# A weight tile rounded before the tanh in the feed-forward's first steps, the key norm's parts ahead of the query's, and in the attention an eviction moved up and a weight split moved behind the loop

## The reference

```python
for l in range(DEPTH):                       # two layers
    h = rmsnorm(x, g_mix[l])
    ...
    if l == 1:
        hk = rmsnorm(x, g_kv)                # the same x under a second gain
        kvf = hk @ w_kvf                     # keys, values, forget logits
        p = h @ w_in_b[0]                    # queries, and the memory's queries
        mix = forgetting_attention(q, k_sh, v_sh, cum_logf)   # 12 heads
    mem_o = memory_attention(q_mem, mem_k, mem_v)             # 4 heads
    x = x + jnp.concatenate([mix, mem_o], axis=-1) @ w_out[l]
    x = x + conv_ffn(rmsnorm(x, g_ffn[l]), w_up[l], w_dw_f[l], b_dw_f[l], w_down[l])

def conv_ffn(h, w_up, w_dw, b_dw, w_down):
    u = causal_dwconv(h @ w_up, w_dw, b_dw)  # three taps over time
    gate, val = jnp.split(u, 2, axis=-1)
    return (jax.nn.silu(gate) * val) @ w_down
```

## Time and profile before

| what | value |
|---|---|
| median of 3 runs | 1224.46 us (1223.63 to 1225.26) |
| the profiled execution's own time | 1224.42 us |
| its span, first to last instruction | 1222.6 us |
| PE busy | 1176.3 us, 96% of the span |
| DVE busy | 854.8 us, 70% |
| ACT busy | 599.6 us, 49% |
| transfers | mean 166 GB/s, the 16 DMA engines 45% busy with the stream |
| mean granted TensorE clock | 0.99 of full |

### The profile page before, as it was taken

The page is one execution under the profiler, slowest core; times in us unless marked ns, Lnnn a source line. Parts: engine busy times, 40 slices in busy tenths (PEclk is TensorE's granted clock), DMA queues, the critical chain, the costliest instruction groups (busy, mean ns, idle before and its releaser), DMA issues.

```text
span 1222.6 us, 19215 instructions
## 1 busy us (share of the span) xinstructions
PE 1176.3 (96%) x7966; PEld 1054.6 (86%) x7966; DVE 854.8 (70%) x1310; ACT 599.6 (49%) x933; POOL 24.6 (2%) x40
## 2 busy tenths in 40 slices
PE   6989998999999999899999999999999999999997
PEld 6958898999899779899999978878799789999885
DVE  5995678787767657887778856665676257777664
ACT  6525545545554435455545334444553245565552
POOL 3000000000000000000000000000000000000000
PEclk9999999999999999999999999999999999999998
DMA  9634444555443314455544544544575522322351
GB/s 378 209 108 158 173 173 174 199 179 179 183 173 118 125 69 173 140 205 177 198 176 152 208 158 149 203 156 155 206 276 207 211 99 99 106 103 104 136 192 50
DMA packets 31398, 202.81 MB, mean 166 GB/s; under 512 B 4048, under 2 KB 4176, under 8 KB 8784
## 3 DMA queue, kind: packets, MB, share of 16 engines
q1 hardware_dynamic: 31312, 201.58, 45.3%
HBM read 198.18 MB, written 1.05 MB: 163 GB/s over the span
## 4 chain that ended last, share of the span: by engine, by line
PE 82%; DVE 9%; ACT 4%; issue 2%; DMA 1%; DVEq 0%; ACTq 0%; POOLq 0%; SPq 0%; POOL 0%
PE bank L792 24%; PE bank L793 23%; PE bank L794 23%; DVE WL L1687 3%; ACT WH L1318 2%; DVE work L1882 2%; PE bank L1292 1%; PE bank L1275 1%; PE bank L1218 1%; PE bank L1182 1%; PE bank L926 1%; PE bank L1006 1%; DMA xn<-cmpw 1%; PE bank L1266 1%; DVE work L1834 1%
## 5 line engine op out<-in xcount | busy, mean ns | idle before, releaser
L1687 DVE TENSOR_TENSOR WL<-RAW,WH 128x2048 fp32r<-128x2048 f32 x172 | 394.8, 2298 | 154.4 <-ACT WH L1318 153.2
L1318 ACT ACTIVATE WH<-RAW 128x2048 fp32r<-128x2048 f32 x172 | 328.5, 1912 | 215.5 <-PE bank L794 207.6
L792 PE MATMUL bank<-XH,WH 128*128 128x256 f32 x1264 | 363.1, 287 | 19.5 <-DVE WL L1903 11.9
L793 PE MATMUL bank<-XL,WH 128*128 128x256 f32 x1264 | 359.5, 284 | 0.0
L794 PE MATMUL bank<-XH,WL 128*128 128x256 f32 x1264 | 359.4, 284 | 0.0
L792 PEld LDWEIGHTS bank<-XH,WH 128*128 128x128 f32 x1264 | 244.4, 193 | 23.6 <-DVE XL L1896 11.8
L793 PEld LDWEIGHTS bank<-XL,WH 128*128 128x128 f32 x1264 | 244.5, 193 | 0.6
L794 PEld LDWEIGHTS bank<-XH,WL 128*128 128x128 f32 x1264 | 244.3, 193 | 0.0
L792 PE MATMUL bank<-WH,MH 128*128 128x512 f32 (+1 forms) x480 | 182.3, 380 | 3.7 <-DVE work L1758 2.7
L793 PE MATMUL bank<-WL,MH 128*128 128x512 f32 (+1 forms) x480 | 179.9, 375 | 0.0
L794 PE MATMUL bank<-WH,ML 128*128 128x512 f32 (+1 forms) x480 | 179.5, 374 | 0.0
(11 more groups left out here) (294 smaller groups left out, 1471.3 us busy)
## 6 DMA issues: line engine op xcount, KB each, us to landing
RAW<-wstream SPq DMA_DIRECT2D x173, 1024.0 KB, 4.8
con<-cmpw SPq DMA_DIRECT2D x6, 512.0 KB, 5.7
xn<-cmpw SPq DMA_DIRECT2D x4, 512.0 KB, 7.6
con<-consts SPq DMA_DIRECT2D x1, 1617.0 KB, 6.7
work<-xT_in SPq DMA_DIRECT2D x1, 1024.0 KB, 4.9
x<-x_in SPq DMA_DIRECT2D x1, 1024.0 KB, 10.8
work<-mem_in SPq DMA_DIRECT2D x1, 1024.0 KB, 15.8
xn<-memT_in SPq DMA_DIRECT2D x1, 1024.0 KB, 13.2
```

What stands on the lines that cost most here:

```text
L792: mm(o, ah, bh, start=start, stop=False)
L793: mm(o, ah, bl, start=False, stop=False)
L1318: act_fn(WH[:, t % RING, :], RAW[:, t % RING, :], ACT.Copy).then_inc(w_rounded, 1)
L1687: tt(WL[:, t % RING, :], RAW[:, t % RING, :], WH[:, t % RING, :].bitcast(F32), ALU.subtract).then_inc(w_split, 1)
```

## The change

Four places are edited; every operation stays, and PE's and SP's lists are the same as before.

1. In `ffn`, ACT and DVE no longer take the extra tile in steps 0 and 1 (the term `0 < 2 * s + q < 2 * LAG` goes). In steps 0, 1 and 2 (s <= LAG) ACT rounds one more tile before it waits for DVE's gate taps and does the tanh; DVE's split of it stands behind the eviction of the value product.
2. In `high` and `low`, with two gains, all four blocks of the half go under the first gain and then all four under the second; ACT waits before each pair of the second for DVE's pair of the first (part_done).
3. In the attention's slot 11, DVE's eviction of qm,1 stands ahead of the maxima and the copy instead of behind them.
4. In slot 16 DVE doesn't split a weight tile any more. The split comes in the call of `enter` that follows the loop.

```diff
             def high(n, h, gains=(0,)):
-                for j in (2 * h, 2 * h + 1):
-                    ready(act, ("tr", n, j))
-                    for dst, _, name in [norms[n][g] for g in gains]:
+                for at, (dst, _, name) in enumerate([norms[n][g] for g in gains]):
+                    for j in (2 * h, 2 * h + 1):
+                        ready(act, ("tr", n, j))
+                        if at:
+                            act.wait_ge(part_done, j + 1)
                         for kk in range(2):
...
                     for q, name in enumerate(("fg", "fv")):
-                        upto_n(at + 1 + q + (0 < 2 * s + q < 2 * LAG))
+                        upto_n(at + 1 + q)
                         is_free(act, (name, l, s))
...
                         if q == 0:
+                            if s <= LAG:
+                                upto_n(at + 2)
                             act.wait_ge(*dve_a.next())
...
             def low(n, h, gains=(0,)):
-                for j in (2 * h, 2 * h + 1):
-                    dve.wait_ge(*hi_a.next(2 * len(gains)))
-                    for g in gains:
-                        hi, dst, name = norms[n][g]
+                for g in gains:
+                    hi, dst, name = norms[n][g]
+                    for j in (2 * h, 2 * h + 1):
+                        dve.wait_ge(*hi_a.next(2))
                         for kk in range(2):
...
-                    if s in pieces:
+                    if s in pieces and s < n:
                         upto(pieces[s][0])
+                    if s in pieces and pieces[s] == (("qm", 1), 1):
+                        by_head(("qm", 1), q_mem)
...
-                        elif name == "qm":
-                            by_head((name, j), q_mem)
...
                         scaled((name, l, s), u[:, 2 * q:2 * q + 2, :])
-                        upto_n(at + 1 + q + (0 < 2 * s + q < 2 * LAG))
+                        upto_n(at + 1 + q)
```

## The result

The changed kernel takes 1207.14 us (median of four executions, 1207.06 to 1208.61) against 1224.86 us before (1223.63 to 1225.33). The ratio is 0.986, with a 95% interval of 0.9843 to 0.9877: 17.7 us less. The profiled execution took 1207.18 us, 17.24 less than the profiled one before (1224.42), its span is 1205.4, and the mean granted clock rose from 0.990 to 0.996.

A forecast was written before the change was run, and what follows sets the result against it. PE, busy 96% of the span, was taken as the bound, each long wait paid twice, as idle time and slow clock. Terms 10.0 + 0.5 + 3.6 + 3.2 = 17.3 us off 1224.4 gave 1207.1, range 1204.8 to 1213.

The forecast's parts named there:

- The feed-forward: Both passes at fv3: the wait for its split (3.42 us) and the slow clock behind it (1.58) go, 10.0 us.
- The norm: Layer 1's norm: keys' parts ready 1.4 us earlier, but q1,0's split limits PE's start; 0.5 us gained.
- Slot 11: Attention, o1,0: earlier eviction of qm,1 starts PE 2.0 us sooner and saves 1.55 of slow clock; 3.6 us together.
- Slot 16: Attention's end: without the split ahead of the copies PE's outputs start 1.5 us earlier, plus 1.7 for the clock; 3.2 us.
- rival D: An early gain, above all the attention's 6.8 us, is used up by a later wait; 1213.9 us, chance 0.04.
- Rival B: A remaining wait of 1.1 us, at the attention's end or q1,0, still lowers the clock; 1208.7 us, chance 0.20.
- C: The feed-forward's split is late still, at worst with about no gain there; 1209 to 1217.1 us, chance 0.12.
- E: Feed-forward steps 0 to 2, both passes: the rounding ahead holds up the tanh; slower, up to 1227.9 us, chance 0.02.
- that rule: Attention's end: transposes don't count as busy, so the clock falls once more; gain 15.6 us instead of 17.3.

The follow-up runs named there:

- no_ffn: Changed kernel with the feed-forward's edit alone undone (extra tile back in steps 0 and 1, no rounding ahead of the tanh): 1217.38 us.
- no_norm: Changed kernel with the two gains' parts interleaved again at layer 1's norm, no wait on part_done: 1207.68 us.
- no_slot11: Changed kernel with the eviction of qm,1 back behind the maxima and the copy of slot 11: 1211.14 us.
- no_slot16: Changed kernel with slot 16's split back in the loop, ahead of the copies: 1210.72 us.
- ffn_drop_only: Changed kernel without the rounding ahead of the tanh in steps 0 to 2; the extra tile stays dropped: 1212.32 us.
- ffn_tanh_only: Changed kernel with the extra tile in steps 0 and 1 back, the rounding ahead of the tanh kept: 1210.77 us.
- norm_split_early: Changed kernel with DVE splitting q1,0 at layer 1's norm behind two additions, ahead of all low parts: 1205.88 us.
- tail_wait_1: Changed kernel plus one extra 128x512 DVE operation ahead of the attention's last copy of transposes, PE's wait 1.65 us: 1208.71 us.
- o1_wait_1: Changed kernel plus two extra 128x448 DVE operations ahead of the eviction of qm,1, PE's wait 1.63 us: 1208.47 us.
- tail_wait_2: Changed kernel plus two extra 128x512 DVE operations ahead of the attention's last copy of transposes, PE's wait 2.25 us: 1210.56 us.
- o1_wait_2: Changed kernel plus three extra 128x472 DVE operations ahead of the eviction of qm,1, PE's wait 2.24 us: 1211.4 us.

## Why the prediction was right

The forecast was 1207.1 us, and the median is 1207.14. The terms were right to some tenths each; that the totals agree to 0.04 us is luck, as executions of one kernel differ by more. Term by term:

**The feed-forward, 10.0 us.** Undoing it costs 10.2. The splits ended where they were worked out: fg3's at 175.13 + 2.29 = 177.42 (177.7), fv3's at 179.87 + 2.28 = 182.15 (182.5), with 2.2 us to spare at fg3 (PE starts it at 179.64). The order of events was right too, as the two halves show: 1.4 and 0.6 us for 1.5 and 0.8, and 1.43 for 1.7. The second term, 1.58 us a pass for the clock, holds as well, since the lateness alone, 3.42 us twice, would make 6.8.

**The norm, 0.5 us.** Right, and for the reason given: the keys' parts come 1.4 us earlier, but q1,0's split is late next. The new wait on part_done, for which 0.1 us was taken, cost 0.19 by DVE's idle time ahead of XL (read from the rows, not tested by itself). In the profiles PE's start of q1,0 moved from 338.58 to 332.91, 0.46 more than the 5.21 by which the last triple of fd10 had moved (331.78 to 326.57).

**Slot 11, 3.6 us.** The start of o1,0 moved from 420.13 to 412.35, 7.78 us, 2.1 of which are this edit's. With the clock it is 3.66 in the trace, and 4.0 by the medians.

**Slot 16, 3.2 us.** From 447.33 to 436.45 is 10.88, 3.1 more than at o1,0: 1.55 for slot 11's clock, which is won behind o1,0's start, and 1.5 for this wait, 2.57 to 1.04. Undoing it costs 3.6 by the medians but 3.07 in the trace, so the term was not too low: the other half us arises ahead of 94 us.

**The sum.** 10.0 + 0.5 + 3.6 + 3.2 = 17.3; by the medians the four undone one at a time give 10.2 + 0.5 + 4.0 + 3.6 = 18.3, and 17.7 was measured for all at once. The traces tell it more closely. All edits lie between two rows of PE that every profile has, transposes in the attention of layer 0 and transposes at the end of the second feed-forward; in the changed kernel these are:

```profile
94.53 0.65 PE L979 MATMUL bank<-ident,work 128*128 128x128 f32 x4
...
633.67 1.03 PE L926 MATMUL bank<-ident,x 128*128 128x128 f32 x8
```

| kernel | first row | second row | from one to the other | more than the changed kernel | worked out ahead |
|---|---|---|---|---|---|
| changed | 94.53 | 633.67 | 539.14 | | |
| before | 94.74 | 651.11 | 556.37 | 17.23 | 17.3 |
| no_ffn | 94.70 | 643.70 | 549.00 | 9.86 | 10.0 |
| no_norm | 94.80 | 634.39 | 539.59 | 0.45 | 0.5 |
| no_slot11 | 95.19 | 637.99 | 542.80 | 3.66 | 3.65 |
| no_slot16 | 95.01 | 637.22 | 542.21 | 3.07 | 3.1 |
| ffn_drop_only | 95.58 | 639.55 | 543.97 | 4.83 | 4.6 |
| ffn_tanh_only | 95.36 | 637.82 | 542.46 | 3.32 | 3.4 |
| norm_split_early | 94.54 | 632.16 | 537.62 | -1.52 | -1.2 |
| tail_wait_1 | 95.51 | 635.26 | 539.75 | 0.61 | 0.6 |
| o1_wait_1 | 95.61 | 635.83 | 540.22 | 1.08 | 1.1 |
| tail_wait_2 | 95.46 | 637.38 | 541.92 | 2.78 | 2.8, with a fall of the clock |
| o1_wait_2 | 95.73 | 638.17 | 542.44 | 3.30 | 3.3, with a fall of the clock |

The four undone add up to 17.04, against 17.23 for all at once. So no later wait uses the gain up (rival D), and PE's waits behind 640 us are those of before, 5.1 us in total against 5.0. The second column shows the spread of 1.2 us that executions bring along from their first 95 us, and that no edit explains.

**Rival B** (a short wait still brings the clock down) did not come true in the profile; the one execution at 1208.61 us, at a mean clock of 0.995 against 0.996, may be such a case; it has no profile. **Rivals C and E** fell with the waits at 0.8 to 1.3 us ahead of each tanh, and with no wait for a split left at fg3 or fv3. The Trainium skill, TensorE: Matmul & The Clock Gate, Part 4: PE-mode transpose, says that transposes don't count as busy in the same way. By that rule the clock was to fall at the attention's end; in the profiles it did not, at a wait of 1.04 us nor at 1.65.

One thing in the argument was passed over: PE's second wait before the change was one of 2.1 us near 55 us, an "issue" row that the list had and the text did not mention. The change doesn't reach it, so no term was wrong for it, but it would have shown that 2 us can go without a fall of the clock. In the kernel before, with the stretch behind it:

```profile
56.73 0.36 PE L792 MATMUL bank<-MH,WH 128*128 128x256 f32 x1 [2.07 <-issue]
```

```profile
57.10:60.50 3.40, 3.40 (x31) 3.40 (x31) 3.36 (x10) 2.44 (x2) 0.00 (x0) 1.00 1.00 323
```

## What to carry to other kernels

Where two engines hand work to each other in turn, look for the idle time ahead of a wait on either side: work that is needed later and can start now (here a rounding of 1.9 us ahead of a tanh that waited 3.1 us) belongs there, and not behind it, where the other engine waits for it. It must be able to start: in ffn_tanh_only a rounding that stood 2.42 us for PE held up taps that were ready. Here a fall of the clock behind a wait of 2.24 us or more cost 1.5 to 1.6 us on top of the wait. When a norm's or an eviction's order changes, ask which tile's weights come next: the split of q1,0 kept two thirds of the gain, and moving it ahead of the low parts on DVE got the rest. And to compare two versions more closely than their medians can, measure in both traces from a row ahead of all edits to one behind them.

## What was not expected of the hardware

The same wait brings the clock down in one execution and not in another. At 55 us, which no edit touches, PE waits 2.05 to 2.08 us in all thirteen profiles; behind it the clock falls to 0.5 in six (the four kernels with added waits, no_ffn and ffn_drop_only) and stays at 1.00 in seven. For one, PE waits 2.05 us in the profile of tail_wait_1 and 2.07 us in the changed kernel's. Behind it the first has

```profile
57.27 0.55 PE L792 MATMUL bank<-MH,WH 128*128 128x256 f32 x1 [2.05 <-issue]
```

```profile
57.10:60.50 3.40, 3.23 (x15) 3.26 (x16) 3.36 (x9) 2.84 (x2) 0.00 (x0) 0.50 0.86 284
```

and the changed kernel

```profile
56.57 0.36 PE L792 MATMUL bank<-MH,WH 128*128 128x256 f32 x1 [2.07 <-issue]
```

```profile
57.10:60.50 3.40, 3.40 (x31) 3.40 (x30) 3.40 (x9) 2.26 (x2) 0.00 (x0) 1.00 0.86 280
```

15 products in 3.4 us against 31. Two waits that differ by 0.02 us have different outcomes. The fall at 90 us varies too: it is in twelve of the profiles and not in no_ffn's, where the clock stands at 1.00 from 90 to 94 us. What decides is not shown. Nor does a fall always cost its 1.6 us: the one at 57 us cost tail_wait_1 nothing, because the waits behind it became shorter by as much. So a single execution's time doesn't tell two versions apart that differ by some 1.5 us.
